# MLP up projections of a two-block kernel on TensorE: four long products together and then four short ones, in place of two and two

## What is computed

```python
def sq_relu_mlp(h, w_in, w_out):
    return jnp.square(jax.nn.relu(h @ w_in)) @ w_out
...
x = x + sq_relu_mlp(rmsnorm(x, mlp_norm_g[layer]), mlp_w_in[layer], mlp_w_out[layer])
```

## Time and profile before

| | |
|---|---|
| time, median of 3 runs | 1394.27 us (1393.8 to 1395.25) |
| the profiled execution | 1393.7 us |
| its span in the profile | 1391.9 us |
| PE busy | 1363.1 us, 98% |
| PEld busy | 1175.4 us, 84% |
| DVE / ACT busy | 950.7 us, 68% / 748.2 us, 54% |
| granted TensorE clock | 9 in each of 40 slices (tenths, 9 is 90% or more) |

### The profile page before, as it was taken

The page is one execution under the profiler, slowest core; times in us unless marked ns, Lnnn a source line. Parts: engine busy times, 40 slices in busy tenths (PEclk is TensorE's granted clock), DMA queues, the critical chain, the costliest instruction groups (busy, mean ns, idle before and its releaser), DMA issues.

```text
span 1391.9 us, 23527 instructions
## 1 busy us (share of the span) xinstructions
PE 1363.1 (98%) x9838; PEld 1175.4 (84%) x9838; DVE 950.7 (68%) x1480; ACT 748.2 (54%) x1262; POOL 62.7 (5%) x63
## 2 busy tenths in 40 slices
PE   6999999999999999999999999999999999999998
PEld 6789888888889778888889877888888898788886
DVE  7896786766675776756667544577666697767665
ACT  6873434555456575545453446555555536555543
POOL 0003440000010000000000000000000100000000
PEclk9999999999999999999999999999999999999999
DMA  9421006555554415555565543545555653455551
GB/s 333 158 72 33 4 27 241 188 185 188 202 205 161 144 49 172 199 186 192 201 221 189 189 162 140 180 156 197 193 185 185 218 174 130 151 183 197 194 185 58
DMA packets 35291, 230.67 MB, mean 166 GB/s; under 512 B 4177, under 2 KB 5505, under 8 KB 8561
## 3 DMA queue, kind: packets, MB, share of 16 engines
q1 hardware_dynamic: 33376, 223.43, 46.6%
q0 software_dynamic: 1808, 5.74, 1.2%
HBM read 228.08 MB, written 1.05 MB: 165 GB/s over the span
## 4 chain that ended last, share of the span: by engine, by line
PE 92%; DVE 5%; ACT 2%; issue 0%; DMA 0%; SPq 0%; DVEq 0%; ACTq 0%
PE bank L1813 18%; PE bank L1814 17%; PE bank L1815 17%; PE bank L1938 17%; PE bank L1941 8%; PE bank L2205 3%; PE bank L1770 1%; PE bank L2011 1%; DVE wlo L999 1%; PE bank L2029 1%; PE bank L2045 1%; PE bank L2222 1%; DVE arena L1227 0%; PE bank L2383 0%; PE bank L2384 0%
## 5 line engine op out<-in xcount | busy, mean ns | idle before, releaser
L999 DVE TENSOR_TENSOR wlo<-raw,whi 128x1024 fp32r<-128x1024 f32 (+1 forms) x416 | 492.9, 1204 | 250.0 <-ACT whi L458 245.7
L458 ACT ACTIVATE whi<-raw 128x1024 fp32r<-128x1024 f32 (+1 forms) x416 | 425.5, 1041 | 329.3 <-PE bank L1815 231.7
L1813 PE MATMUL bank<-whi,XHL 128*128 128x512 f32 x872 | 342.3, 393 | 0.0
L1814 PE MATMUL bank<-wlo,XHL 128*128 128x512 f32 x872 | 339.6, 389 | 0.0
L1815 PE MATMUL bank<-whi,XHL 128*128 128x512 f32 x872 | 339.5, 389 | 0.0
L1938 PE MATMUL bank<-XHL,whi 128*128 128x512 f32 x1008 | 316.6, 395 | 0.2
L1941 PEld LDWEIGHTS bank<-XHL,wlo 128*128 128x128 f32 x1008 | 189.3, 188 | 44.5
L1941 PE MATMUL bank<-XHL,wlo 128*128 128x256 f32 x1008 | 198.1, 278 | 0.0
L1815 PEld LDWEIGHTS bank<-whi,XHL 128*128 128x128 f32 x872 | 163.7, 188 | 34.3
L1813 PEld LDWEIGHTS bank<-whi,XHL 128*128 128x128 f32 x872 | 163.7, 188 | 34.2 <-issue 1.7
L1814 PEld LDWEIGHTS bank<-wlo,XHL 128*128 128x128 f32 x872 | 163.8, 188 | 32.7 <-issue 0.5
(11 more groups left out here) (302 smaller groups left out, 1265.3 us busy)
## 6 DMA issues: line engine op xcount, KB each, us to landing
raw<-in_w_mlp SPq DMA_DIRECT2D x128, 1024.0 KB, 4.9
raw<-in_w_rv SPq DMA_DIRECT2D x8, 1024.0 KB, 4.9
raw<-in_w_rg SPq DMA_DIRECT2D x8, 1024.0 KB, 4.9
raw<-in_w_reo SPq DMA_DIRECT2D x8, 1024.0 KB, 5.0
raw<-in_w_k SPq DMA_DIRECT2D x4, 1024.0 KB, 9.6
raw<-in_w_v SPq DMA_DIRECT2D x4, 1024.0 KB, 9.8
raw<-in_w_r SPq DMA_DIRECT2D x4, 1024.0 KB, 4.9
raw<-in_w_rwo SPq DMA_DIRECT2D x4, 1024.0 KB, 5.0
```

Of the source, the lines that this page charges most:

```text
L458: act.activation(high, full, ACT.Copy).then_inc(hi_done, 1)
L999: dve.tensor_tensor(low, full, high, ALU.subtract).then_inc(lo_done, 1)
L1813: pe.matmul(out_, xh[xs], wh[ws], start=start, stop=False)
L1814: pe.matmul(out_, xh[xs], wl[ws], start=False, stop=False)
```

## The change

The loop over the four tiles of half a unit becomes a loop over two pairs of tiles. For a pair the four long products are issued first (tile a twice, tile b twice), then the four short ones. Every product keeps its operands, its bank and its place in the sum of its bank; the semaphore counts, and the instructions of all other engines, stay what they were. The waits keep their place among the long products. The signals of a tile hang on its last short product, as before. In `after` the long products stand on L1937.

```diff
--- before.py
+++ after.py
@@ -1926,24 +1926,25 @@
                             continue
                         if j == 0:
                             pe.wait_ge(turned_lo, SPLIT0[TI[name]] + kt // 2 + 1)
-                        for f in range(UK):
-                            t = 4 * j + f
-                            bank = psum[up_bank(t)]
-                            if kt == 0 and t >= 6:
-                                pe.wait_ge(up_sum, t0 + (t - 5 if t < 8 else t - 3))
-                            if t == 2 and kt == 0 and i < 2:
-                                feed(name, 1)
-                            cols = slice(f * P, (f + 1) * P)
-                            for e in range(2):
-                                pe.matmul(bank[:, :], whi[:, u % SPLIT_RING, k2 + e, cols],
-                                          XHL[:, kt + e].rearrange("p h t -> p (h t)"), start=(kt + e == 0), stop=False)
-                            for e in range(2):
-                                ins = pe.matmul(bank[:, 0:T], wlo[:, u % SPLIT_RING, k2 + e, cols], XH[:, kt + e],
-                                                start=False, stop=(kt + e == KT - 1))
-                            if f == UK - 1:
-                                ins.then_inc(unit_used, 1)
-                            elif kt + 2 == KT:
-                                ins.then_inc(up_done, 1)
+                        for pair in ((0, 1), (2, 3)):
+                            for f in pair:
+                                t = 4 * j + f
+                                if kt == 0 and t >= 6:
+                                    pe.wait_ge(up_sum, t0 + (t - 5 if t < 8 else t - 3))
+                                if t == 2 and kt == 0 and i < 2:
+                                    feed(name, 1)
+                                for e in range(2):
+                                    pe.matmul(psum[up_bank(t)][:, :], whi[:, u % SPLIT_RING, k2 + e, f * P:(f + 1) * P],
+                                              XHL[:, kt + e].rearrange("p h t -> p (h t)"), start=(kt + e == 0), stop=False)
+                            for f in pair:
+                                for e in range(2):
+                                    ins = pe.matmul(psum[up_bank(4 * j + f)][:, 0:T],
+                                                    wlo[:, u % SPLIT_RING, k2 + e, f * P:(f + 1) * P], XH[:, kt + e],
+                                                    start=False, stop=(kt + e == KT - 1))
+                                if f == UK - 1:
+                                    ins.then_inc(unit_used, 1)
+                                elif kt + 2 == KT:
+                                    ins.then_inc(up_done, 1)
 
                 def down(u, n, j):
                     if n == 0:
```

## The result

| | before | with the change |
|---|---|---|
| time, median | 1394.27 us | 1398.03 us |
| lowest to highest of 11 runs each | 1393.13 to 1395.25 | 1396.45 to 1400.09 |
| the profiled execution, and its span | 1393.7, 1391.9 us | 1397.29, 1395.4 us |

The ratio is 1.0027, 95% interval 1.0019 to 1.0035: slower by 2.6 to 4.9 us. The forecast was 1396.1 with a range to 1398.2; the time lies at the range's upper end, above the narrower band of 1395.2 to 1397.2, and on the far side of the 0.2% (1397.06).

What follows compares the result with a forecast made beforehand. The prediction took TensorE's product pace, not waits, as the bound. Pairs add 1.8 us, boundaries cancel and late tiles cost nothing: 1395.5 us for the profiled execution, 1396.1 us for the median, range 1393.0 to 1398.2.

Steps and rivals of the forecast that it cites:

- the narrower band: Total time between 1395.2 and 1397.2 us, where the forecast was said to hold, with chance 0.58.
- the 0.2%: Smallest difference a measurement can tell, 2.8 us; slower beyond it (above 1397.06 us) was given 0.22.
- What bounds the kernel: TensorE holds 92% of the chain that ended last; the reordered up projection loops have no wait to remove, only product pace.
- the late tiles: First tile of each pair ends 0.47 us later; covers over 2 us, cost nothing; chance of a TensorE wait 0.03.
- Four longs behind shorts: Up projections: a run of four long products after short ones takes 0.93 us, a surcharge of 0.023 us.
- Four shorts: Up projections: a run of four short products behind longs takes 0.47 us, with one credit of about 0.01 us.
- The term of +0.007 us a pair: Up projections: a pair of tiles takes 1.40 us, 0.007 more than before; over 252 pairs, 1.8 us more.
- The boundaries cancel: Between up and down steps, 28 of each kind: 0.5 us gained at first pairs, 0.5 us lost in down steps.
- The rival in which order does not matter: Up projections: four-and-four costs what two-and-two does, so time stays 1394.3 us; chance 0.20.
- the forget gate: Loop alternating one long and one short product, 0.348 us for both; cited as evidence that order is free.
- The shorts that profit: Up projections: weights load ahead during longs, so all four shorts run faster; 3.3 us less, 1391.0 us; chance 0.07.
- The lost credit: Up projections: shorts behind unsettled longs all cost 0.12 us, a pair 1.41; 4.3 us more, 1398.6 us; chance 0.12.

Runs made afterwards that it cites:

- pace_alone: A kernel of its own computing nothing of the reference: TensorE alone runs products in long runs and cycles of widths; four and four of 512 and 256 took 1.403 us.
- the repetition: The changed kernel measured once more without any edit: 1399.24 us beside 1394.15 of the kernel before, ratio 1.0032.

## Why the prediction came out as it did

**What bounds the kernel** held: pace, no wait. No idle time appeared, and the late tiles cost nothing, shown by their own experiment.

**Four longs behind shorts, 0.93 us**, held (0.93 measured). **Four shorts, 0.47**, held at the resolution of the timeline (0.47 to 0.48; their share is 1.403 - 0.929 = 0.474). But the sum of the two rounded terms is 1.40, and a pair takes 1.403; the kernel before takes 1.393 in the settled part of a step. The term of +0.007 us a pair was therefore +0.010, and its 1.8 us over 252 pairs would be 2.4. What failed is the size, for a reason that the prediction names itself: two terms read to 0.01 us each, to find a difference of 0.007.

**The boundaries cancel** failed. The gain at the first pair of an up step is 0.004 (1.379 us against 1.383 by the starts in ns), not the 0.010 that I gave it. It is also had 24 times and not 28, since step 1 begins behind the up step of step 0 and not behind a down step. The loss of the down step, which does come 28 times, is 0.037, not 0.02: the prediction priced it by longs behind a settled run of shorts, but behind runs of four the longs are not settled and the surcharge runs on for nine products. Together 24 up steps behind a down step cost 24 x 0.063 = 1.5 us, 28 down steps 28 x 0.037 = 1.0, and the first two up steps of each MLP 0.5 more: 3.0, where I had 1.8.

**The rival in which order does not matter** rested on the forget gate. Runs of one are dearer than runs of two in the MLP (0.353 against 0.348), so the row was misleading. A price by columns alone falls with it: the cycles of `pace_alone` show up to 0.020 us a turn on top, which depends on the neighbours. The Trainium skill, page "TensorE: Matmul & The Clock Gate", section "Back-to-back issue gap", gives a gap that goes by columns alone for an isolated product; for the products in this stream the traces do not agree with it. **The shorts that profit** did not come. **The lost credit** came in part: the first short behind four such longs takes 118 ns, behind settled longs 113, and four shorts take 0.471 and 0.478 us in turn, 0.474 in the mean, beside the 0.47 of the earlier trace rows.

**The 0.2%**: 3.0 us of pace is just past 2.8, where I had given 0.22. The remaining 0.8 us of the median goes for the most part with the granted clock of the runs, which I did not reckon with at all; whether the order has a part in it is not settled. That 1398.03 lies inside the range owes something to luck: the upper part of the range was there for the lost credit, not for down steps and clock, and the five runs of the repetition have a median of 1399.24, outside it.

## What to carry to other kernels

On an engine that never waits, read the price of an order from the distance of starts over whole repetitions, and measure a repetition of the new order if the trace holds one; two terms rounded to 10 ns cannot carry a difference of 7. Fewer turns between two kinds of products need not be cheaper: here turns cost 3 ns at runs of two and 17 to 20 ns from runs of four on, so grouping lost although it halved their number. What stands behind the changed loop inherits its state and belongs in the sum.

## What the runs showed of the hardware

In these runs a matmul's pace depends on the widths of its neighbours. Between products of one width it is steady (0.2267 us at 512 columns, 0.120 at 256); behind a change from 256 or 384 columns to 512, about five products of 512 are slower by 2 to 9 ns each, 0.020 us net with the credit of the first shorts (113 and 119 ns in place of 120). The price is the same behind one short product as behind eight, it does not depend on banks (tried with runs of two), nor on which of two weight tiles is loaded, and it vanishes when both kinds have 512 columns. The same slow products follow a change of pace from 0.427 us within one width (`pace_alone`), so they are not peculiar to a change of width. What the two cases have in common, and why runs of two are nearly free of it, the runs do not show.

From 192 columns down the pace stays at 0.111 us, so something other than the moving columns sets it there. By the Trainium skill, page "TensorE: Matmul & The Clock Gate", section "LDWEIGHTS (loading the stationary operand)", the time of a load goes by its columns; worked out from its formula, the estimate for 128 columns is 107 ns, which would fit the floor. No run here separates the two.
